# Input chunks of two token mixers: one full-precision product against three products of rounded halves

## The reference, cut to what matters

```python
def token_mixer(h, w_in, w_out, ...):
    qkv_a, a_a, b_a, z_a, qkv_b, qk_c, v_c, i_c, f_c, o_c = jnp.split(h @ w_in, IN_SPLITS, axis=-1)
    ...   # gated delta rule (a), block attention (b), mLSTM (c)
    return jnp.concatenate([oa, ob, hc], axis=-1) @ w_out

def first_block(x, c, ...):
    for l in range(DEPTH):
        mod = (jax.nn.silu(c) @ ada_w[l] + ada_b[l]).reshape(b_, N_SUB, 3, D_MODEL)
        y = swiglu(modulate(x, mod[:, 0, 0], mod[:, 0, 1]), ffn_w13[l, 0], ffn_w2[l, 0])
        x = layer_norm(ALPHA * x + 0.5 * (1 + mod[:, 0, 2])[:, None, :] * y, ln_g[l, 0], ln_b[l, 0])
        y = token_mixer(modulate(x, mod[:, 1, 0], mod[:, 1, 1]), w_in[l], w_out[l], ...)
        x = layer_norm(ALPHA * x + (1 + mod[:, 1, 2])[:, None, :] * y, ln_g[l, 1], ln_b[l, 1])
        y = swiglu(modulate(x, mod[:, 2, 0], mod[:, 2, 1]), ffn_w13[l, 1], ffn_w2[l, 1])
        ...
```

## Time and profile before

| | us |
|---|---|
| median of three executions | 1979.32 |
| the profiled execution | 1980.76 |
| its span | 1979.0 |
| TensorE busy in the span | 1880.8 |
| VectorE busy | 1243.6 |
| ScalarE busy | 696.1 |
| GpSimd busy | 130.4 |
| first mixer's first projections, start to end of chunk 6 | 250.31 to 304.10 |
| second mixer with its output projection | 913.87 to 1148.17 |

### The profile page before, as it was taken

The page is one execution under the profiler, slowest core; times in us unless marked ns, Lnnn a source line. Parts: engine busy times, 40 slices in busy tenths (PEclk is TensorE's granted clock), DMA queues, the critical chain, the costliest instruction groups (busy, mean ns, idle before and its releaser), DMA issues.

```text
span 1979.0 us, 30724 instructions
## 1 busy us (share of the span) xinstructions
PE 1880.8 (95%) x13040; PEld 1592.9 (80%) x13040; DVE 1243.6 (63%) x2232; ACT 696.1 (35%) x929; POOL 130.4 (7%) x68
## 2 busy tenths in 40 slices
PE   6999999998999989998999989998999998989997
PEld 4999988877999989998888789998744555436896
DVE  3887655535887687665672469997794665125712
ACT  2433243233533263334332363332521333024322
POOL 0000063300000000004430000000000000000000
PEclk9999999989999999999999999999999998999999
DMA  9777623422577646663334037765351201112100
GB/s 391 286 271 260 236 107 128 172 86 107 219 260 287 242 161 242 250 237 140 135 137 184 22 149 274 278 247 203 110 209 64 86 1 66 45 62 85 65 22 22
DMA packets 47256, 323.81 MB, mean 164 GB/s; under 512 B 4960, under 2 KB 8160, under 8 KB 8336
## 3 DMA queue, kind: packets, MB, share of 16 engines
q1 hardware_dynamic: 47120, 321.85, 43.0%
HBM read 320.78 MB, written 1.05 MB: 163 GB/s over the span
## 4 chain that ended last, share of the span: by engine, by line
PE 86%; DVE 8%; ACT 3%; issue 1%; SPq 1%; DMA 1%; DVEq 0%; ACTq 0%
PE ps L336 85%; DVE wk L1778 3%; ACT wk L1298 2%; DVE wk L1775 2%; PE ps L339 1%; DVE wk L1772 1%; SPq L1274 1%; DVE low L1772 1%; DMA ring<-in_stream_dram 1%; ACT L1298 1%; DVE xa L1775 0%; DVE xlo L1772 0%; DVE tab L1772 0%; ACT xa L1298 0%; DVE wk L1781 0%
## 5 line engine op out<-in xcount | busy, mean ns | idle before, releaser
L336 PE MATMUL ps<-xa,ring 128*128 128x256 f32 (+1 forms) x1776 | 485.5, 432 | 18.2 <-ACT xa L1298 11.6
L336 PEld LDWEIGHTS ps<-xa,ring 128*128 128x128 f32 x1776 | 338.6, 193 | 150.7 <-issue 103.9
L336 PE MATMUL ps<-xhi,low 128*128 128x256 f32 x1408 | 387.9, 283 | 0.0
L336 PE MATMUL ps<-xhi,whi_wk 128*128 128x256 f32 x1088 | 306.9, 293 | 19.3 <-ACT xhi L1298 12.4
L1298 ACT ACTIVATE wk<-ps 128x256 f32<-128x256 f32 (+4 forms) x221 | 109.8, 504 | 583.0 <-PE ps L336 497.7
L336 PE MATMUL ps<-xlo,whi_wk 128*128 128x256 f32 x1088 | 297.5, 282 | 0.0
L336 PEld LDWEIGHTS ps<-xhi,low 128*128 128x128 f32 x1408 | 262.9, 190 | 0.0
L1298 ACT ACTIVATE whi_wk<-ring 128x2048 fp32r<-128x2048 f32 x100 | 191.0, 1914 | 201.7 <-DMA ring<-in_stream_dram 115.0
L1778 DVE SCALAR_TENSOR_TENSOR wk<-ring,sc,wk 128x256 f32<-128x256 f32 x576 | 234.0, 477 | 0.0
L336 PE MATMUL ps<-wk 64*64 64x64 f32 (+10 forms) x2712 | 223.4, 270 | 6.7 <-ACT wk L1298 5.1
L1772 DVE TENSOR_TENSOR low<-ring,whi_wk 128x2048 fp32r<-128x2048 f32 x100 | 228.1, 2284 | 0.3 <-ACT whi_wk L1298 0.3
(11 more groups left out here) (108 smaller groups left out, 2404.9 us busy)
## 6 DMA issues: line engine op xcount, KB each, us to landing
ring<-in_stream_dram SPq DMA_DIRECT2D x302, 1024.0 KB, 5.9
tab<-in_tab_dram SPq DMA_DIRECT2D x1, 1376.0 KB, 24.0
res<-in_xt_dram SPq DMA_DIRECT2D x1, 1024.0 KB, 23.1
res<-in_ct_dram SPq DMA_DIRECT2D x1, 1024.0 KB, 8.7
out_dram<-wk SPq DMA_DIRECT2D x2, 512.0 KB, 3.0
tab<-in_tab_dram SPq DMA_DIRECT2D x1, 256.0 KB, 2.9
cols<-in_cols_dram SPq DMA_DIRECT2D x1, 242.5 KB, 2.6
tab<-in_wg_dram SPq DMA_DIRECT2D x1, 96.0 KB, 2.0
```

What stands on the lines that cost most here:

```text
L336: last[0] = nc.tensor.matmul(o, l, r, start=start, stop=stop, skip_group_check=free)
```

## The change

1. In `project`, each product of a mixer chunk becomes three: high weights by high input, low by high, high by low. `x_hi` and `x_lo` lie in the two halves of `xa`'s memory (`whi_xa`). Chunk 0 has its own order, `project_first`: all pieces high by high, then low by high, then high by low.
2. Each of the sixteen chunks takes two ring places. ScalarE rounds the chunk from the first into the second (`rounded`), at places in its program set by hand (`ROUND_AT` and calls in `norm` and `mixer`). GpSimd subtracts in the first place, so that the low half lies there. The second place is marked `("rounded",)` in the order, and SyncE loads nothing for it; `loads(n)` counts loads of a place.
3. GpSimd no longer has modulation work. VectorE forms the sums of the eight ada chunks in their ring place (`mod_part`, nine instructions), between solve steps 4 and 5, after step 6, and ahead of two norms. `MOD_AT` puts the column sums at slots 21 to 45 and the eighth behind `early`; `MIXER_ADA` loads the chunks later; `modulation(m + 1)` moves to `norm`.
4. Before a mixer ScalarE writes the rounded input, all eight pieces; VectorE writes all eight in full, then the eight low pieces over them.
5. The block attention's output goes to `res` and not to `xa`, the mLSTM's mean to banks 5 and 6.

```diff
@@ -46,7 +46,9 @@
-MOD_AT = {3: 2, 7: 3, 13: 4, 17: 5, 21: 6, 25: 7}
+WIN = WIN_FIRST + WIN_LATER
+MOD_AT = {21: 0, 23: 1, 25: 2, 27: 3, 29: 4, 31: 5, 45: 6}
+ROUND_AT = {10: 11, 14: 12, 17: 13, 24: 14, 34: 15}
@@ -146,6 +148,10 @@
+        def loads(n):
...
+            return 16 * sum(1 for i in range(n % RING, n + 1, RING) if order[i] != ("rounded",))
@@ -270,7 +276,11 @@
-        MIXER_ADA = {0: 0, 1: 1, 3: 2, 4: 3, 6: 4, 8: 5, 10: 6, 11: 7}
+        MIXER_ADA = {11: (0, 1), 13: (2, 3), 14: (4, 5, 6, 7)}
...
+        def win_no(l, i):
...
+            return found["chunk_no", "win", l, WIN[i]][1]
@@ -351,13 +353,23 @@
-                eng.wait_ge(landed[n % RING], 16 * (n // RING + 1))
+                eng.wait_ge(landed[n % RING], loads(n))
...
+            def take_both(*tag):
...
+                held[0] = n = len(order)
+                found[("chunk_no",) + tag] = ("", n)
+                order.append(tag)
+                order.append(("rounded",))
+                return n
...
+                if held[0] + 1 < len(order) and order[held[0] + 1] == ("rounded",):
+                    found["chunk", held[0] + 1] = found["chunk", held[0]]
@@ -492,20 +504,47 @@
-                def project(o, w, ch, t, first=False):
+                x_hi, x_lo = whi_xa[:, :, CS], whi_xa[:, :, XS]
...
+                def project(o, w, ch, t):
...
+                    hi, lo = w
...
-                        if first:
-                            eng.wait_ge(*step_of("xmt", m, k))
...
-                            mm(o, w[:, k, P * t:P * t + P], xa[:, k, XS], k == 0, k == KT - 1)
+                            at = slice(P * t, P * t + P)
+                            mm(o, hi[:, k, at], x_hi[:, k, :], k == 0, False)
+                            mm(o, lo[:, k, at], x_hi[:, k, :], False, False)
+                            mm(o, hi[:, k, at], x_lo[:, k, :], False, k == KT - 1)
...
-                            mm(o, xa[:, k, T + P * t:T + P * t + P], w[:, k, 0:o.shape[1]], k == 0, k == KT - 1)
+                            at, n = slice(P * t, P * t + P), o.shape[1]
+                            mm(o, x_hi[:, k, at], hi[:, k, 0:n], k == 0, False)
+                            mm(o, x_hi[:, k, at], lo[:, k, 0:n], False, False)
+                            mm(o, x_lo[:, k, at], hi[:, k, 0:n], False, k == KT - 1)
...
+                def project_first(w):
...
+                    hi, lo = w
+                    at = [slice(0, P), slice(P, 2 * P)]
+                    o = [bank(1, 0, 256), bank(1, 256, 512)]
+                    for k in range(KT):
+                        eng.wait_ge(scalar_done, step("xh", m, k))
+                        for t in range(2):
+                            mm(o[t], hi[:, k, at[t]], x_hi[:, k, :], k == 0 and t == 0, False, free=True)
+                    eng.wait_ge(gpsimd_done, step("wlow", l, 0))
+                    for k in range(KT):
+                        for t in range(2):
+                            mm(o[t], lo[:, k, at[t]], x_hi[:, k, :], False, False, free=True)
+                    for k in range(KT):
+                        eng.wait_ge(vector_done, step("xl", m, k))
+                        for t in range(2):
+                            mm(o[t], hi[:, k, at[t]], x_lo[:, k, :], False, k == KT - 1, free=True)
...
-                    w = tiles(take("win", l, ch), 256)
-                    if i in MIXER_ADA:
-                        leave("ada", m + 1, MIXER_ADA[i])
-                    return w
+                    n = take_both("win", l, ch)
+                    eng.wait_ge(*(step_of("wlow", l, i) if i else step_of("wround", l, i)))
+                    for c in MIXER_ADA.get(i, ()):
+                        leave("ada", m + 1, c)
+                    return tiles(low[:, (n + 1) % RING, :], 256), tiles(low[:, n % RING, :], 256)
@@ -595,12 +632,13 @@
-                    for t in range(2):
-                        project(bank(1 + i, 256 * t, 256 * t + 256), w, ch, t, i + t == 0)
+                    if i == 0:
+                        project_first(w)
+                    else:
+                        for t in range(2):
+                            project(bank(1 + i, 256 * t, 256 * t + 256), w, ch, t)
...
-                    if i == 2:
-                        mod_cols(m + 1, 0)
@@ -609,7 +647,6 @@
-                        mod_cols(m + 1, 1)
@@ -795,6 +836,7 @@
                 early(0, 1)
+                mod_cols(m + 1, GATE - 1)
                 eng.wait_ge(vector_done, step("mixed", m))
@@ -1268,10 +1310,14 @@
-            for n in range(stream.shape[0]):
+            rows = 0
+            for n, tag in enumerate(order):
+                if tag == ("rounded",):
+                    continue
...
-                eng.dma_start(ring[:, n % RING, :], stream[n]).then_inc(landed[n % RING], 16)
+                eng.dma_start(ring[:, n % RING, :], stream[rows if marks else 0]).then_inc(landed[n % RING], 16)
+                rows += 1
@@ -1318,13 +1362,21 @@
-                eng.wait_ge(landed[n % RING], 16 * (n // RING + 1))
+                eng.wait_ge(landed[n % RING], loads(n))
...
+            def rounded(l, i):
...
+                n = win_no(l, i)
+                eng.wait_ge(landed[n % RING], loads(n))
+                eng.wait_ge(*step_of("chunk", n + 1 - RING))
+                act(low[:, (n + 1) % RING, :], ring[:, n % RING, :], ACT.Copy, "wround", l, i).then_inc(scalar_done, 1)
...
+                o = whi_xa[:, :, CS] if m % 3 == 1 else xhi
...
-                    act(xhi[:, t, :], i[:, t], ACT.Identity, "xh", m, t, scale=scale[:, t:t + 1], bias=bias[:, t:t + 1]).then_inc(scalar_done, 1)
+                    act(o[:, t, :], i[:, t], ACT.Identity, "xh", m, t, scale=scale[:, t:t + 1], bias=bias[:, t:t + 1]).then_inc(scalar_done, 1)
@@ -1358,6 +1410,9 @@
                     whole(m + 1, 0)
+                elif m < 5:
+                    rounded(m // 3, 0)
+                    rounded(m // 3, 1)
                 for q in range(4):
@@ -1369,16 +1424,14 @@
+                for q in range(4):
+                    eng.wait_ge(vector_done, step("xn", m, q))
+                    highs(m + 1, tiles(ff_cen, 256), co[:, 16:24], co[:, 24:32], range(2 * q, 2 * q + 2))
...
-                    for q in range(4):
-                        eng.wait_ge(vector_done, step("xn", m, q))
-                        highs(m + 1, tiles(ff_cen, 256), co[:, 16:24], co[:, 24:32], range(2 * q, 2 * q + 2))
...
-                    for q in range(2):
-                        eng.wait_ge(vector_done, step("xn", m, q))
-                        affine(m, xa[:, :, XS], tiles(ff_cen, 256), co[:, 16:24], co[:, 24:32], range(2 * q, 2 * q + 2), ("xm_a0", "xm_a")[q], m + 1)
+                    rounded(m // 3, 2)
@@ -1472,8 +1525,11 @@
+                        if s in ROUND_AT:
+                            rounded(l, ROUND_AT[s])
...
+                rounded(l, 3)
@@ -1485,8 +1541,12 @@
                     silu(t)
+                    if t % 2 and t < 5:
+                        rounded(l, 4 + t // 2)
                 eng.wait_ge(scalar_done, done.count)
                 act(g_sq, W(QKV, 1536), ACT.Square, "l2sq", m).then_inc(scalar_done, 1)
+                rounded(l, 6)
+                rounded(l, 7)
                 eng.wait_ge(vector_done, step("l2e", m))
@@ -1495,6 +1555,7 @@
                 fill(2)
+                rounded(l, 8)
                 eng.wait_ge(tensor_done, step("pairs", m))
@@ -1508,6 +1569,7 @@
                         act(g_dt[:, u], g_dt[:, u], ACT.Exp, *(("dt", m) if h + c == 6 else ()), bias=colt[:, c, h:h + 1]).then_inc(scalar_done, 1)
+                rounded(l, 9)
                 fill(3)
@@ -1516,6 +1578,7 @@
                 act(g_kdt, bank(6, 0, 384), ACT.Copy, "vbt_read", m).then_inc(scalar_done, 1)
+                rounded(l, 10)
                 fill(20)
@@ -1784,17 +1847,15 @@
-                vecs = [i for i in range(1 if m < 6 else 2) if i not in by_gpsimd(m, ch)]
-                if not vecs:
-                    return
+                vecs = range(1 if m < 6 else 2)
...
-                acc = mod_acc(m, ch)
+                acc = w if in_slot(m, ch) else mod_acc(m, ch)
...
-                if mod_before(m, ch) is not None:
+                if not in_slot(m, ch) and mod_before(m, ch) is not None:
...
-                eng.wait_ge(landed[n % RING], 16 * (n // RING + 1))
+                eng.wait_ge(landed[n % RING], loads(n))
@@ -1804,9 +1865,12 @@
+                eng.wait_ge(vector_done, done.count)
+                if in_slot(m, ch):
+                    tt(w[:, 0], w[:, 0], w[:, 1], ADD, "modsum", m, ch).then_inc(vector_done, 1)
+                    return
...
-                eng.wait_ge(vector_done, done.count)
@@ -1867,11 +1931,12 @@
+                hi, o = (whi_xa[:, :, CS], whi_xa[:, :, XS]) if m % 3 == 1 else (xhi, xlo)
...
-                    tt(xlo[:, t, :], xa[:, t, XS], xhi[:, t, :].bitcast(F32), SUB, "xl", m, t).then_inc(vector_done, 1)
```

(26 more changed lines are left out.)

36 lines of the change are left out of this document (6 added, 30 removed).

## The result

The changed kernel takes **2026.23 us** (median of four executions, 2023.75 to 2029.55) against 1979.9 us before: the ratio is 1.0236, with a 95% interval of 1.0218 to 1.0253. Forecast were 1956 us, in a range of 1937 to 1974. The kernel became slower by 46 us where 24 us were to be gained.

The account below looks back on a forecast made before the run. TensorE's instruction stream was taken as the bound. Per mixer 18.8 us saved less 2.0, 1.0, 0.5, 2.1, 1.0 and 0.3 gives 11.9, 23.8 for two: from 1980.76 to 1957.0, median 1.4 lower, so 1956 us, range 1937 to 1974.

Parts of the forecast that it names:

- the three places that I listed: GpSimd slowing VectorE: input's low halves (2.0 us), SwiGLU tail (1.0 us), modulation part under chunk 14's subtraction (1.0 us).
- product, 14 chunks: TensorE's three products of rounded halves save 1.34 us a chunk, 18.8 us per mixer.
- first chunk, input's low half: Start of a mixer: GpSimd slows VectorE's last low halves, first chunk ends later; 2.0 us lost (0 to 3.5).
- end of the SwiGLU: Feed-forward tail before a mixer: two GpSimd subtractions slow VectorE's modulation, normalisation 0.8 us late; 1.0 us lost (0 to 2.5).
- row work and pairs: VectorE's scans and short instructions before TensorE's pairs: no loss counted; chunks 6 and 7 ready 2 us or more ahead.
- chunk 4: First projections: ScalarE rounds it behind two silus, ready near 276.1 against TensorE's 276.4; 0.5 us lost.
- chunk 14: During the solve: rounded only behind ScalarE's copy of mo1, so TensorE waits for GpSimd; 2.1 us lost.
- modulation parts: VectorE's eight parts, 3.5 us each: 1.0 us lost where chunk 14's subtraction overlaps one, 0.3 us for parts 6 and 7.
- q15: Last chunk, 128 columns: 48 matmuls take 3.8 us against 3.84 before, no change (ends -0.7 and +1.9 us).
- the second rival (rounding paces): ScalarE's rounding queue late at two more chunks of each mixer, 3 us each: 12 us worse, 1968 us; chance 0.23.
- VectorE becomes the bound: GpSimd slows all six parts in the solve to 8.2 us each: 18.9 us lost per mixer, 2017 us; chance 0.10.
- the likeliest case: The summed forecast of 1956 us, spanning 1949 to 1963 by the ends of q15, start and tail; chance 0.42.

Follow-up runs that it names:

- experiment 1: Changed kernel with GpSimd subtracting only 64 of 2048 columns of each mixer chunk, the low-by-high product reading the rounded place (work left out): 1956.85 us.
- experiment 11: Changed kernel with VectorE forming seven chunks' low halves and half of chunk 6's, roundings moved, GpSimd gated for chunk 7, ScalarE's gate ahead of the root: 1961.24 us.
- Experiment 8: Kernel before the change with each of GpSimd's 64 modulation instructions cut to 64 columns (work left out): 1978.86 us, against 1981.49 beside it.
- experiment 5: Changed kernel with VectorE instead of GpSimd forming the low halves of chunks 0 and 1 of each mixer: 2015.15 us.
- experiment 3: Changed kernel without the multiplies and adds of VectorE's eight modulation parts in each mixer, only the last addition kept (work left out): 2012.23 us.
- experiment 10: Changed kernel with the second half of chunk 6 multiplied four times over, to fill TensorE's wait for the row work: 2021.01 us.
- experiments 8 and 12: The first is Experiment 8; the second is the kernel before the change with only ScalarE's gate edit: 1981.2 us, ratio 1.0005.

## Why the prediction was wrong

**The step that failed** is the price of GpSimd beside VectorE. I read the 0.97 and 1.55 us of the earlier trace rows as a slowing "to less than half speed", multiplied by it at the three places that I listed, and put nothing for VectorE's row work. The runs showed in its place a full halt until GpSimd's instruction ends: 4.98 us for a scan of 0.68 us, with some 65 of the 69 us between after and experiment 1 back once the halts lay elsewhere (experiment 11). Experiment 8 shows what the 0.97 and 1.55 us were: rests of GpSimd's instructions, met at a random point. Before's additions take 2.4 and 1.3 us, so the rests were short, and any ratio taken from them small. A subtraction of 4.7 us has long rests. The trace of before even had a longer one, under GpSimd's multiply of 3.60 us (362.79 to 366.39), for a pair that takes 0.55 us elsewhere:

```profile
363.66 3.09 DVE L1775 TENSOR_SCALAR wk<-wk,small 128x128 f32<-128x128 f32 x2
```

No factor of two fits that row. The size of the price follows from GpSimd's instruction, not from VectorE's.

The terms of the sum, one by one (us per mixer, first mixer):

| term | forecast | measured |
|---|---|---|
| product, 14 chunks | +18.8 | about +16 |
| first chunk, input's low half | -2.0 | stood still 4.4 of 7.13 us; TensorE's wait 3.31 |
| end of the SwiGLU | -1.0 | -5.9 from 222.00 us on, -7.7 from the same product on; experiment 5 gives 8.1 back |
| row work and pairs | 0 | -16: 13.8 longer, though its products save 2.3 |
| chunk 4 | -0.5 | no wait in after |
| chunk 14 | -2.1 | -2.62, and 2.3 more at the low clock |
| modulation parts | -1.3 | part 0 7.8 us, part 3 7.7 us (forecast 3.5); -7 by experiment 3 |
| q15 | 0 | -1.74 |

- *The product.* This is TensorE in before, a half chunk:

```profile
307.37 3.72 PE L336 MATMUL ps<-xa,ring 128*128 128x256 f32 x16
```

and 3.13 us in after: 0.59 us a half, 1.2 a chunk and not 1.34; a row of four halves in after's first projections takes 11.86 us, where two chunks took 14.06. Mechanism right, size some 13% too high: the pace of the long row would give 2.84 us for 24 matmuls.
- *The end of the SwiGLU and the start.* The overlap of the instructions was found rightly, the price not: VectorE's group of six is 8.7 us longer, and I had it 0.8 us late.
- *The row work.* This place was not in the sum at all. I had asked only when chunks 6 and 7 are ready for TensorE ("ready 2 us or more ahead"), which was right, and not what VectorE does while GpSimd makes them. It is the most costly place, since here TensorE has nothing else to do.
- *q15.* Measured 5.58 us for 48 matmuls, 116 ns each: a product of halves costs the same with 128 columns as with 256. I had the row that says so as an upper bound and chose 3.8, near the lower one.
- *Chunk 14.* Predicted as a wait of about 2 us for GpSimd ahead of its first half; the row says 2.62 <-POOL.
- *ScalarE* kept its times: the second rival (rounding paces) is not seen.

The nearest rival was "VectorE becomes the bound", 2017 us, and its rule from the Trainium skill, page "GPSIMD Engine Reference", section "8. Key points", names just this contention; the trace agrees, with a size that the page doesn't give. I placed it in the six parts with a factor of 2.4, and gave it 10% because "GpSimd has just two subtractions in that stretch". That its 2017 us lie near the 2026 measured is luck: it has 21 us more in that stretch, which became 5.8 us longer. Luck has a part in the 1956.85 us of experiment 1 too, which is my 1956: there the product saves less than I had, q15 costs 1.74 us, and the losses that I counted at the start, at chunk 14 and in the parts are gone. One sum is wrong as well: with all the upper ends that I name (1.9, 1.5 and 1.5 us, twice) the likeliest case reaches 1966, not 1963. The right count was over all sixteen subtractions, at each asking which instruction of VectorE starts under it and who waits for that.

**What stays open** is the clock. The low stretch behind the row work costs some 6 us of a mixer (after: 5.91 + 5.23 + 4.63 us against 3.17 + 3.13 + 3.13); the two levels are 1.2 and 2.4 GHz, and the granted 0.50 in the first row is the lower one. In the first mixer it came behind waits of 9.84, 5.43, 3.62, 2.77 and 1.25 us, and not behind 0.40 and 0.25 us. In the second mixer it came, in part, behind 0.40 and 0.20 us too, while behind 1.49 us the row of twelve was spared (experiment 10), and the kernel before has one such half chunk there behind no wait of that kind:

```profile
967.64 3.17 PE L336 MATMUL ps<-wk,tab 32*128 32x256 f32 x12
970.74 5.41 PE L336 MATMUL ps<-xa,ring 128*128 128x256 f32 x16
```

That half chunk takes 3.72 us in the traces of experiments 8 and 12, whose TensorE program is the same, so the clock at this place differs between executions of nearly the same kernel. Filling the wait did not hold it in both mixers. What in this stretch decides it, no run here tells.
